# Expert weights in a ring of three thirds: two transfers of 6 MB an expert from one array, in place of three of 4 MB

## The chip, the cores and the metric

One core of one Trainium2 chip runs the whole layer. The metric is the device time in microseconds, the median over runs of the same kernel. MB stands here for 2^20 bytes, except in the profile's own rows, which count 10^6 bytes to a MB.

## What is computed

```python
n = rms_norm(x, norm1_w); proj = n @ w_in            # q, k, v and u: 256 tokens, width 1024
a = sliding_window_attention(q, k, v, sinks)         # 8 query heads, 2 key heads, window 128
p = multiscale_pool(u, pool_w, pool_scale)
h = x + concat(a, p) @ w_out
# mixture of experts: 32 experts, the best 4 for each token, all in float32
logits = rms_norm(h) @ w_router + b_router
gu = xb @ w_gu[e] + b_gu[e]                          # w_gu[e] 1024 x 2048
act = min(gate, 7) * sigmoid(1.702 * gate) * (clip(up, -7, 7) + 1)
y = act @ w_down[e] + b_down[e]                      # w_down[e] 1024 x 1024
h = h + segment_sum(y * gate_weight)
```

All 32 experts get tokens, so every weight is read once from HBM: 12 MB an expert, 384 MB in all, beside some 13 MB for the layer's first half.

## The kernel before

**Pieces and the ring.** An expert's weights are six pieces of 2 MB (`PIECES`), each 16 KB a partition: pieces 0 to 3 hold gate and up, 4 and 5 hold down. A gate-up piece is two chunks of 128 rows by 2048 columns, a down piece four chunks of 128 by 1024. The weights live in `ring`, which has 8 slots (`RING`), and piece number s (expert times 6 plus piece) goes to slot s mod 8. After the first three experts `load_pair` fills two slots with one transfer of 4 MB, 32 KB a partition, so an expert is three transfers: two from `w_gu`, one from `w_down`. SP (SyncE) issues all of them on one queue. Before each it waits on `pieces_used`, which TensorE raises when it has used up a piece: `load_pair(s)` needs `s + 2 - 8` pieces used.

**Loading ahead.** Buffers of the first half that are free early take parts of late experts (`ahead`): the first chunk of experts 24 to 29 (1 MB each; `AHEAD = 6`), four of the twelve half-MB blocks in the tile `extra`, and the first down chunk of experts 24 and 25 (`down_ahead`, 0.5 MB each). These experts' transfers are shorter by as much. In the first half of the program SP loads single pieces and halves of pieces as slots come free (`BY_CHUNK`, `SINGLES = 14`).

**TensorE's order.** `expert` does, for one expert of up to 64 tokens: `gate_up` (eight chunks, then the bias), `between` (gather of tokens for a later expert, `to_tokens`, which adds the last expert's result to the tokens' sums, `turn_round`, which transposes the activations once VectorE and ScalarE have made them, and `turn_gates`), and `down` (eight chunks). `wait_landed` stands at pieces 0, 2 and 4, one wait a transfer. Experts 0 to 3 are unrolled, then come eight short matmuls for the bias of down (line 1378), a loop of four experts run five times, and eight experts unrolled. The last two experts (30 and 31) are interleaved: both `gate_up` first, then both `down`, and SP loads them in that order (`LAST_TWO`) and, from piece 2 of expert 30 on, cut small (`END_CUTS`, each cut with a semaphore of its own, `landed_end`), down to 0.5 MB.

**The end.** After the last down chunk `to_tokens` of expert 31 closes the sums, ScalarE and VectorE copy them out and three transfers store them.

```python
            for s in range(RING + 2, 3 * TP - 2 * PIECES, 2):
                sp.wait_ge(pieces_used, (TURNS - 3) * TP + s + 2 - RING)
                gu_ahead = 0 <= s - TP < AHEAD * PIECES and s % PIECES == 0
                load_pair(s, NE - 3 * TURN, 2 * FF if gu_ahead else DM if s in (TP + GU_PIECES, TP + PIECES + GU_PIECES) else 0)
```

The functions that the diff touches, and what calls them:

Of the kernel before, what the change touches and what calls it, by code (L numbers as in the profile page):

```python
# [29 lines left out]
P = 128  # L30
SEQ, DM = 256, 1024
# [34 lines left out]
END_CUTS = {(2, 2): ((4, 6), (6, 8)), (3, 0): ((0, 2), (2, 4)), (3, 2): ((4, 6), (6, 7), (7, 8)),  # L66
            (2, 4): ((0, 2), (2, 4), (4, 6), (6, 7), (7, 8)), (3, 4): ((0, 2), (2, 4), (4, 6), (6, 7), (7, 8))}
# [5 lines left out]
AHEAD = 6  # L73
# [43 lines left out]
def laid_out(inputs):  # L117
# [8 lines left out]
    def one_by_one(a, stops):  # L126
# [29 lines left out]
        "w_gu": w_gu.reshape(NE, 2, 4, P, 2, 2, 2, FF // 4).transpose(0, 1, 3, 2, 5, 6, 4, 7).reshape(NE * 2, P, PAIR),  # L156
        "w_down": w_down.reshape(NE, 8, P, DM).transpose(0, 2, 1, 3).reshape(NE, P, PAIR),
# [4 lines left out]
def layer_kernel(nc, x_tok, x_dim, first, second, third, fixed, bands, w_qkv, w_u, w_mix, w_pool, b_gu, b_down,  # L162
                 w_gu, w_down, out):
    out_t = out.rearrange("b (t p) d -> (b t) p d", p=P)
    w_gu_k = w_gu.rearrange("s p n -> p s n")
    w_dn_k = w_down.rearrange("s p n -> p s n")

    with ExitStack() as ctx:
# [25 lines left out]
        extra = sb("extra", [P, 4, 1024])  # L194
# [17 lines left out]
        def cut(n, of=passing):  # L212
# [67 lines left out]
            mixA[:, :, :].rearrange("p h s -> p (h s)"), bias[:, 0, :], U[:, :, :].rearrange("p t n -> p (t n)"), bias[:, 1, :], passing[:, 0:1024],  # L280
            *(extra[:, n, :] for n in range(4)))]
# [3 lines left out]
        down_ahead = [mixP[:, :, :].rearrange("p g s -> p (g s)"), xT[:, FF:2 * FF]]  # L285
# [19 lines left out]
        landed_end = {(u, c, k): sem(f"landed_end{u}_{c}_{k}") for (u, c), parts in END_CUTS.items() for k, _ in parts}  # L305
        ld_aside = [sem(f"ld_aside{k}") for k in range(2)]
        ld_ahead = [sem(f"ld_ahead{u}") for u in range(AHEAD)]
        ld_wout, ld_bdn, ld_bgu = sem("ld_wout"), sem("ld_bdn"), sem("ld_bgu")
        ld_down_ahead = [sem(f"ld_down_ahead{u}") for u in range(2)]
        landed = [sem(f"landed{c}") for c in range(RING // 2)]  # L310
# [30 lines left out]
        gt_psum, gt_sb, y_sb = sem("gt_psum"), sem("gt_sb"), sem("y_sb")  # L341
        more_done = sem("more_done")
# [21 lines left out]
        def _(sp):  # L364
# [51 lines left out]
            def load_down_ahead(u):  # L416

                sp.dma_start(down_ahead[u], w_dn_k[:, NE - 2 * TURN + u, 0:DM]).then_inc(ld_down_ahead[u], 16)
# [1007 lines left out]
```

## Time and profile before

| | |
|---|---|
| median of 3 runs | 988.81 us (988.5 to 988.91) |
| the profiled execution's own time | 988.7 us |
| its span in the profile | 986.9 us |
| TensorE busy | 946.6 us, 96% |
| 16 DMA engines, mean busy share | 9 in tenths in 39 of 40 slices |
| VectorE, ScalarE busy | 202.9 us, 127.7 us |
| HBM read | 416.80 MB (of 10^6 bytes) |

Two resources are busy almost without a break, so a busy share alone does not tell which one sets the end. The span is 1.8 us shorter than the execution's own time; what lies around it does not change with the order of the work. In the rows, an engine with a q (SPq) is that engine's sequencer, and "DMA ring<-w_gu_dram" in a chain is the time from the issue of a transfer to its landing.

### The profile page before, as it was taken

The numbers are of one execution on the slowest core, as the hardware profiler recorded it, in microseconds if no ns is written. First come the engines' busy times: TensorE is split into PE (matmuls) and PEld (weight loads), VectorE is DVE, ScalarE is ACT, GpSimd is POOL, SyncE is SP. The second block draws the span as 40 slices with busy tenths as digits, with TensorE's granted clock in tenths as the row PEclk, the third lists the DMA queues.
The fourth block names the chain that finished last, engine by engine and source line by source line (L and its number), as shares of the span: only waits on it lengthen the run. The fifth ranks groups of instructions, "written<-read, shape, count | busy, mean of one in ns | idle before, by whom it ended". The sixth has DMA issues, their size and how long they took to land.

```text
span 986.9 us, 11112 instructions
## 1 busy us (share of the span) xinstructions
PE 946.6 (96%) x4508; PEld 382.4 (39%) x4508; DVE 202.9 (21%) x610; ACT 127.7 (13%) x346; POOL 14.0 (1%) x9
## 2 busy tenths in 40 slices
PE   9999999999999899898989989889989999999997
PEld 5545433333333334333333333333333333333432
DVE  4645121212111121210112121011212112111121
ACT  2433111011110111010011101001101110011101
POOL 0031000000000000000000000000000000000000
PEclk9999999999999999999999999999999999999999
DMA  9999999999999999999999999999999999999996
GB/s 374 426 423 398 412 429 434 432 430 428 432 431 429 436 430 430 434 432 429 434 433 426 437 432 428 437 430 429 436 429 431 432 429 430 431 433 430 422 422 272
DMA packets 23869, 418.27 MB, mean 424 GB/s; under 512 B 2912, under 2 KB 3296, under 8 KB 8224
## 3 DMA queue, kind: packets, MB, share of 16 engines
q1 hardware_dynamic: 23408, 417.20, 99.2%
q10 hardware_dynamic: 432, 0.66, 0.2%
q8 instruction: 21, 0.34, 0.1%
q14 instruction: 8, 0.07, 0.0%
HBM read 416.80 MB, written 1.05 MB: 423 GB/s over the span
## 4 chain that ended last, share of the span: by engine, by line
PE 63%; DMA 36%; DVE 1%; issue 0%; ACT 0%; SPq 0%; DVEq 0%
DMA ring<-w_gu_dram 33%; PE ps L1237 29%; PE ps L1342 14%; PE ps L1205 4%; PE ps L1189 4%; DMA ring<-w_down_dram 3%; PE ps L1066 3%; PE ps L997 2%; PE ps L1004 1%; PE ps L1293 1%; PE ps L1301 1%; PE ps L1013 0%; PE ps L1039 0%; PE ps L1058 0%; PE ps L1046 0%
## 5 line engine op out<-in xcount | busy, mean ns | idle before, releaser
L1237 PE MATMUL ps<-ring,passing 128*64 128x512 f32 x1008 | 229.1, 604 | 14.8 <-DMA ring<-w_gu_dram 14.8
L1237 PE MATMUL ps<-ring,PR 128*64 128x512 f32 x976 | 224.5, 608 | 16.4 <-DMA ring<-w_gu_dram 16.2
L1342 PE MATMUL ps<-ring,PT 128*64 128x512 f32 x984 | 218.3, 595 | 0.5 <-DMA ring<-w_down_dram 0.5
L952 DVE TENSOR_SCALAR xw<-ps 128x256 f32<-128x256 f32 x64 | 27.2, 425 | 650.0 <-PE ps L1237 650.0
L1237 PEld LDWEIGHTS ps<-ring,passing 128*64 128x64 f32 x1008 | 76.8, 139 | 158.3 <-issue 143.8
L1237 PEld LDWEIGHTS ps<-ring,PR 128*64 128x64 f32 x976 | 74.9, 140 | 157.0 <-issue 145.4
L1342 PEld LDWEIGHTS ps<-ring,PT 128*64 128x64 f32 x984 | 68.1, 137 | 129.6 <-issue 127.5
L652 ACT ACTIVATE xw<-xw 128x256 f32<-128x256 f32 x64 | 26.6, 416 | 484.5 <-DVE xw L952 484.5
L1205 PE MATMUL ps<-PT 64*128 64x512 f32 x248 | 69.7, 640 | 0.0
L1189 PEld LDWEIGHTS ps<-qk,X 128*128 128x128 f32 x512 | 59.6, 191 | 18.8 <-issue 18.8
L1189 PE MATMUL ps<-qk,X 128*128 128x128 f32 x512 | 65.7, 281 | 0.0
L647 ACT COPY PT<-ps 128x512 f32<-128x512 f32 x31 | 18.1, 585 | 202.7 <-PE ps L1342 202.7
L965 DVE COPY PT<-ps 128x512 f32<-128x512 f32 x31 | 21.4, 692 | 41.5 <-PE ps L1293 41.5
L953 DVE TENSOR_SCALAR ps<-ps 128x256 f32<-128x256 f32 x64 | 27.0, 423 | 0.0
L923 DVE TENSOR_SCALAR qk<-C,qk 128x128 f32<-128x128 f32 x66 | 19.9, 344 | 28.3 <-PE ps L1301 28.3
L1237 PE MATMUL ps<-bgs,oneh 96*64 96x512 bf16 x128 | 25.5, 380 | 0.0
L957 DVE SCALAR_TENSOR_TENSOR ps<-ps,xw 128x256 f32<-128x256 f32 x64 | 24.1, 423 | 0.0
L961 DVE TENSOR_TENSOR xw<-ps,xw 128x256 f32<-128x256 f32 x64 | 23.9, 415 | 0.0
L1205 PEld LDWEIGHTS ps<-PT 64*128 64x128 f32 x248 | 18.7, 184 | 11.1 <-issue 7.6
L1293 PEld LDWEIGHTS ps<-C,xw 128*128 128x128 f32 x128 | 13.4, 140 | 24.3 <-issue 23.2
L997 PE MATMUL ps<-ring,xw 128*128 128x512 f32 (+1 forms) x64 | 22.3, 512 | 0.0
L1293 PE MATMUL ps<-C,xw 128*128 128x128 f32 x128 | 21.0, 286 | 0.5 <-DVE xw L961 0.5
(198 smaller groups left out, 374.6 us busy)
## 6 DMA issues: line engine op xcount, KB each, us to landing
ring<-w_gu_dram SPq DMA_DIRECT2D x48, 4096.0 KB, 28.2
ring<-w_down_dram SPq DMA_DIRECT2D x25, 4096.0 KB, 29.7
ring<-w_gu_dram SPq DMA_DIRECT2D x14, 2048.0 KB, 14.2
ring<-w_gu_dram SPq DMA_DIRECT2D x6, 3072.0 KB, 23.2
ring<-w_down_dram SPq DMA_DIRECT2D x5, 2048.0 KB, 23.1
ring<-w_gu_dram SPq DMA_DIRECT2D x9, 1024.0 KB, 9.6
ring<-w_down_dram SPq DMA_DIRECT2D x8, 1024.0 KB, 25.9
ring<-w_down_dram SPq DMA_DIRECT2D x2, 3584.0 KB, 27.6
```

Source lines behind the costliest of these rows:

```text
L652: nc.scalar.activation(sg[:, b, :], gb[:, b, :], ACT.Sigmoid, scale=ALPHA).then_inc(sig_ready, 1)
L952: nc.vector.tensor_scalar(gb[:, b, :], gu[:, b, 0, :], LIMIT, None, ALU.min).then_inc(g_ready, 1)
L953: nc.vector.tensor_scalar(gu[:, b, 1, :], gu[:, b, 1, :], LIMIT, -LIMIT, ALU.min, ALU.max).then_inc(u_ready, 1)
L957: nc.vector.scalar_tensor_tensor(gu[:, b, 1, :], gu[:, b, 1, :], 1.0, gb[:, b, :], ALU.add, ALU.mult).then_inc(ug_ready, 1)
L961: nc.vector.tensor_tensor(gb[:, b, :], gu[:, b, 1, :], sg[:, b, :], ALU.mult).then_inc(act_ready, 1)
L997: last = mm(ps[:, bank, 0:w], tT[:, k, t * P:(t + 1) * P], wqkv[:, k, a:a + w], start=k == 0, stop=k == KC - 1)
L1066: last = mm(ps[:, ACC[t] + c, :], src[:, h, t * P:(t + 1) * P], wout[:, first + h, 512 * c:512 * c + 512], start=first == 0 and h == 0, st ...
L1189: last = mm(ps[:, bank, k * P:(k + 1) * P], X[:, t, (4 * h + k) * P:(4 * h + k + 1) * P], S1[:, t, :], start=k == 0 and t == 0, stop=t == ...
L1205: return [mm(ps[:, ACC[t] + j, :], GT[64 * j:64 * j + 64, t, :], ye[64 * j:64 * j + 64, :], start=False, stop=True, skip_group_check=True) ...
L1237: last = mm(ps[64 * j:64 * j + 64, GU + b, :], lhs, halves[j][:, 512 * b:512 * b + 512], start=start, stop=stop)
L1293: last = nc.tensor.transpose(ps[:, bank, r * P:(r + 1) * P], gb[:, r // 2, r % 2 * P:(r % 2 + 1) * P], ident)
L1342: last = mm(ps[64 * j:64 * j + 64, bank, :], at[:, k, 64 * (c - GU_PIECES):64 * (c - GU_PIECES) + 64], rows[:, 512 * j:512 * j + 512], sta ...
```

## The change

The ring has nine slots, in three thirds of 6 MB (48 KB a partition). `w_gu` and `w_down` are laid out as one array, `w_all`, whose row 2e holds pieces 0 to 2 of expert e and row 2e + 1 pieces 3 to 5. `load_part` fills a third with one transfer and needs `3 * (part + 1) - 9` pieces used. TensorE waits at pieces 0 and 3. The fill before the loop ends with single pieces 18 to 20 (`SINGLES = 12`), so part 7 (pieces 21 to 23) is the first whole third. The tile `extra` goes; `ahead` serves experts 26 to 29, and the two blocks of `down_ahead` now hold the first chunk of piece 3 of expert 26 (`later_ahead`). TensorE runs experts 0 and 1, a loop of twelve experts run twice, then the bias matmuls, then experts 26 to 31. The last down chunk of expert 31 is loaded, multiplied, copied and added to the tokens' sums in two column halves.

```diff
-RING = 8
+RING = 9
...
-LAST_TWO = [(2, c) for c in range(GU_PIECES)] + [(3, c) for c in range(GU_PIECES)] + [(u, c) for u in (2, 3) for c in range(GU_PIECES, PIECES)]
 PIECE = 4096
-PAIR = 2 * PIECE
-FIRST_FILL = (1, 2, 2, 3)
-BY_CHUNK, SINGLES = (RING, RING + 1, RING + 3), 14
-MORE_LANDINGS, LATER_LANDINGS = (3, 1, 3, 1), (1, 1, 1, 0)
-END_CUTS = {(2, 2): ((4, 6), (6, 8)), (3, 0): ((0, 2), (2, 4)), (3, 2): ((4, 6), (6, 7), (7, 8)),
...
+PART = 3
+TRIPLE = PART * PIECE
+SLOTS_OF = RING // PART
+HALVES = NE * 2
+FIRST_PLACE = (NE - 2) * PIECES
+LAST_TWO = [(e, c) for e in (NE - 2, NE - 1) for c in range(GU_PIECES)] + [(e, c) for e in (NE - 2, NE - 1) for c in range(GU_PIECES, PIECES)]
+BY_CHUNK, SINGLES = (RING, RING + 1, RING + 3), 12
+LANDINGS = (2, 3, 4, 4, 6, 3, 3)
+END_CUTS = {(NE - 2, 0): ((0, 4),), (NE - 2, 2): ((4, 6), (6, 8)), (NE - 1, 0): ((0, 2), (2, 4)), (NE - 1, 2): ((4, 6), (6, 7), (7, 8)),
+            (NE - 2, 4): ((0, 2), (2, 4), (4, 6), (6, 7), (7, 8)), (NE - 1, 4): ((0, 2), (2, 4), (4, 6), (6, 7))}
+LAST_COLUMNS = ((0, 256), (256, 512))
...
-AHEAD = 6
+AHEAD = 4
+AHEAD_FROM = NE - 2 - AHEAD
+ROUND_PARTS, ROUND_EXPERTS = 12, 12
...
-        "w_gu": w_gu.reshape(NE, 2, 4, P, 2, 2, 2, FF // 4).transpose(0, 1, 3, 2, 5, 6, 4, 7).reshape(NE * 2, P, PAIR),
-        "w_down": w_down.reshape(NE, 8, P, DM).transpose(0, 2, 1, 3).reshape(NE, P, PAIR),
+        "w_all": np.concatenate([w_gu.reshape(NE, 8, P, 2, 2, 2, FF // 4).transpose(0, 2, 1, 4, 5, 3, 6).reshape(NE, P, GU_PIECES * PIECE),
+                                 w_down.reshape(NE, 8, P, DM).transpose(0, 2, 1, 3).reshape(NE, P, (PIECES - GU_PIECES) * PIECE)],
+                                2).reshape(NE, P, 2, TRIPLE).transpose(0, 2, 1, 3).reshape(HALVES, P, TRIPLE),
...
-        extra = sb("extra", [P, 4, 1024])
...
-            *(extra[:, n, :] for n in range(4)))]
...
-        down_ahead = [mixP[:, :, :].rearrange("p g s -> p (g s)"), xT[:, FF:2 * FF]]
+        later_ahead = [mixP[:, :, :].rearrange("p g s -> p (g s)"), xT[:, FF:2 * FF]]
...
-            def load_pair(s, first=0, skip=0):
-
-                slot, e, c = s % RING, first + s // PIECES, s % PIECES
-                src, row = (w_gu_k, e * 2 + c // 2) if c < GU_PIECES else (w_dn_k, e)
-                load(slot, row, src, skip, PAIR).then_inc(landed[slot // 2], 16)
...
+            def load_part(part, skip=0, rounds=0):
+
+                slot = part % SLOTS_OF
+                load(rounds + part, slot, skip).then_inc(landed[slot], 16)
...
-            load_pair(0)
+            load_piece(0, stop=2 * PIECE)
             load_piece(RING + 2)
-            for n in range(8, 2 * AHEAD):
-                load_ahead(n)
+            load_piece(RING - 1)
...
-            load_down_ahead(0)
+            load_later_ahead(0)
-                    load_down_ahead(1)
+                    load_later_ahead(1)
...
-            for s in range(RING + SINGLES, RING + 2 + TP, 2):
-                sp.wait_ge(pieces_used, s + 2 - RING)
-                load_pair(s)
-            with sp.Fori(1, TURNS - 3) as r:
-                for s in range(RING + 2, RING + 2 + TP, 2):
-                    sp.wait_ge(pieces_used, r * TP + s + 2 - RING)
-                    load_pair(s, r * TURN)
-            for s in range(RING + 2, 3 * TP - 2 * PIECES, 2):
-                sp.wait_ge(pieces_used, (TURNS - 3) * TP + s + 2 - RING)
-                gu_ahead = 0 <= s - TP < AHEAD * PIECES and s % PIECES == 0
-                load_pair(s, NE - 3 * TURN, 2 * FF if gu_ahead else DM if s in (TP + GU_PIECES, TP + PIECES + GU_PIECES) else 0)
...
+            first_part = (RING + SINGLES) // PART
+            with sp.Fori(0, 3) as r:
+                for part in range(first_part, first_part + ROUND_PARTS):
+                    sp.wait_ge(pieces_used, r * (PART * ROUND_PARTS) + PART * (part + 1) - RING)
+                    load_part(part, rounds=r * ROUND_PARTS)
+            for part in range(first_part + 3 * ROUND_PARTS, HALVES - 4):
+                sp.wait_ge(pieces_used, PART * (part + 1) - RING)
+                begun = part >= 2 * AHEAD_FROM and (part % 2 == 0 or part == 2 * AHEAD_FROM + 1)
+                load_part(part, 2 * FF if begun else 0)
...
+                if (e, first_c) == (NE - 1, GU_PIECES):
+                    part, first, at = place_of(KC - 1)
+                    ends = ring[:, at:at + DM].rearrange("p (j n) -> p j n", j=2)
+                    rows = w_k[:, part, first:first + DM].rearrange("p (j n) -> p j n", j=2)
+                    for q, (a, b) in enumerate(LAST_COLUMNS):
+                        sp.dma_start(ends[:, :, a:b], rows[:, :, a:b]).then_inc(landed_cols[q], 16)
...
-            down_out(NE - 1, 0, GU + 1, ye_last)
+            act.wait_ge(pieces_used, NE * PIECES)
+            for done, (a, b) in zip((y_first, y_sb), LAST_COLUMNS):
+                nc.scalar.copy(ye_last[:, a:b], ps[:, GU + 1, a:b]).then_inc(done, 1)
...
-                    s = place(c)
-                    pair = s % RING // 2
-                    fills = FIRST_FILL[pair] + s // RING
-
-                    if not (isinstance(turn, int) and turn == 0) or s >= RING:
-                        fills += MORE_LANDINGS[pair]
-                    if not (isinstance(turn, int) and turn == 0) or s >= 2 * RING:
-                        fills += LATER_LANDINGS[pair]
+                    part = 2 * e + c // PART
                     if step == "more":
-                        fills -= (1, 1, 1, 2)[pair]
-                    pe.wait_ge(landed[pair], turn * (16 * TP // RING) + 16 * fills)
-
+                        pe.wait_ge(landed_more[c // PART], later * (16 * TURN) + 16 * (e + 1 - NE))
+                        return
+                    fills = sum(LANDINGS[m] if m < len(LANDINGS) else 1 for m in range(part % SLOTS_OF, part + 1, SLOTS_OF))
+                    pe.wait_ge(landed[part % SLOTS_OF], rounds * (16 * 2 * ROUND_EXPERTS // SLOTS_OF) + 16 * fills)
...
+                        begun = early is not None and c == 0 or early == 0 and c == PART
+                        if not last_two and not begun and c % PART == 0:
                             wait_landed(c)
...
-                        elif c == GU_PIECES and k == first_ahead:
-                            wait_landed(c)
...
 
-            for u in range(TURN):
-                if u == 1:
-                    pe.wait_ge(GdT_sb, 1)
-                expert(0, u, "first" if u == 0 else None)
-
+            expert(0, "first")
+            pe.wait_ge(GdT_sb, 1)
+            expert(1)
+            with pe.Fori(0, 2) as r:
+                for e in range(2, 2 + ROUND_EXPERTS):
+                    expert(e, rounds=r)
             pe.wait_ge(ld_bdn, 16)
-            pe.wait_ge(GdT_sb, 1)
             for t in range(T):
                 for c in range(2):
                     mm(ps[:, ACC[t] + c, :], GdT[c * NE:(c + 1) * NE, t, :], bdn[c * NE:(c + 1) * NE, :], start=False, stop=True, skip_group_check=True)
-            with pe.Fori(1, TURNS - 2) as r:
-                for u in range(TURN):
-                    expert(r, u)
-            for u in range(TURN):
-                expert(TURNS - 2, u, early=u)
-
-            for u in range(TURN - 2):
-                expert(TURNS - 1, u, early=TURN + u)
-            gate_up, between, _, _, down = expert(TURNS - 1, TURN - 2, "last but one")
+            for u in range(AHEAD):
+                expert(AHEAD_FROM + u, early=u)
...
-            pe.wait_ge(y_sb, NE)
             for t in range(T):
-                for last in to_tokens(t, GT_last, ye_last):
-                    last.then_inc(acc_final, 1)
+                for q, (a, b) in enumerate(LAST_COLUMNS):
+                    pe.wait_ge(*((y_first, 1), (y_sb, NE))[q])
+                    for j in range(2):
+                        last = mm(ps[:, ACC[t] + j, a:b], GT_last[64 * j:64 * j + 64, t, :], ye_last[64 * j:64 * j + 64, a:b],
+                                  start=False, stop=True, skip_group_check=True)
+                        if b == 512:
+                            last.then_inc(acc_final, 1)
```

Of the two orders, first **SP at the late experts**: before, its issues from expert 29 on. The names `w_gu_dram`, `w_down_dram` and `w_all_dram` are the weight arrays in HBM; 8192 columns are 4 MB, 12288 are 6 MB.

```order
L397 DMA ring<-w_gu_dram 128x6144 [waits pieces_used]
L397 DMA ring<-w_gu_dram 128x8192 [waits pieces_used]
L397 DMA ring<-w_down_dram 128x8192 [waits pieces_used]
L397 DMA ring<-w_gu_dram 128x8192 [waits pieces_used]
L397 DMA ring<-w_gu_dram 128x4096 [waits pieces_used]
L397 DMA ring<-w_gu_dram 128x4096
```

And now, the issues after the loop:

```order
L405 DMA ring<-w_all_dram 128x12288 [waits pieces_used] x9
L405 DMA ring<-w_all_dram 128x10240 [waits pieces_used] x3
L405 DMA ring<-w_all_dram 128x12288 [waits pieces_used]
L405 DMA ring<-w_all_dram 128x10240 [waits pieces_used]
L405 DMA ring<-w_all_dram 128x12288 [waits pieces_used]
L405 DMA ring<-w_all_dram 128x10240 [waits pieces_used]
L405 DMA ring<-w_all_dram 128x12288 [waits pieces_used]
L405 DMA ring<-w_all_dram 128x8192 [waits pieces_used]
L405 DMA ring<-w_all_dram 128x4096 [waits pieces_used]
L405 DMA ring<-w_all_dram 128x4096
```

Three transfers an expert have become two, and the short ones (10240 columns) are 5 MB. The cut transfers at the end stand as before, but for the last 0.5 MB, which comes in two column halves.

Second, **TensorE at one late expert**, from its first chunk, which is taken from the ahead buffers: expert 29 before,

```order
L1237 MATMUL ps<-extra,PR 64x512 [waits ld_ahead5,xe_sb]
L1237 MATMUL ps<-extra,PR 64x512 x3
L1237 MATMUL ps<-ring,PR 64x512 [waits landed3]
L1237 MATMUL ps<-ring,PR 64x512 x11
L1237 MATMUL ps<-ring,PR 64x512 [waits landed0,xe_sb]
L1237 MATMUL ps<-ring,PR 64x512 x11
```

and now expert 29 again (`ps` is PSUM, `PR` and `passing` hold the gathered tokens, `bias` and `passing` ahead blocks):

```order
L1243 MATMUL ps<-bias,PR 64x512 [waits ld_ahead3,xe_sb]
L1243 MATMUL ps<-passing,PR 64x512
L1243 MATMUL ps<-bias,PR 64x512
L1243 MATMUL ps<-passing,PR 64x512
L1243 MATMUL ps<-ring,PR 64x512 [waits landed1]
L1243 MATMUL ps<-ring,PR 64x512 x11
L1243 MATMUL ps<-ring,PR 64x512 [waits xe_sb]
L1243 MATMUL ps<-ring,PR 64x512 x7
L1243 MATMUL ps<-ring,PR 64x512 [waits landed2]
L1243 MATMUL ps<-ring,PR 64x512 x3
```

Before, TensorE waited for a transfer ahead of piece 0 (its second chunk), of piece 2 and, further down, of the down chunks. Now the second wait (`landed2`) stands ahead of piece 3, and none ahead of down.

Third, **TensorE behind the loop**: the bias matmuls (line 1378 before, 1385 now) stood ahead of expert 4, and now stand ahead of expert 26:

```order
L1379 REGISTER_ALU
L1379 COMPARE_AND_BRANCH
L1385 MATMUL ps<-PT 128x512 [waits ld_bdn]
L1385 MATMUL ps<-PT 128x512 x3
L1243 MATMUL ps<-spare,passing 64x512 [waits ld_ahead0,xe_sb]
```

## Rows read from the trace of the kernel before

**Rows 1.** The page: busy time, and DMA rate in 40 slices.

```profile
PE 946.6 (96%) x4508; PEld 382.4 (39%) x4508; DVE 202.9 (21%) x610; ACT 127.7 (13%) x346; POOL 14.0 (1%) x9
...
GB/s 374 426 423 398 412 429 434 432 430 428 432 431 429 436 430 430 434 432 429 434 433 426 437 432 428 437 430 429 436 429 431 432 429 430 431 433 430 422 422 272
```

**Rows 2.** Chain of waits, the middle: start us, us, what.

```profile
397.94 31.45 DMA ring<-w_gu_dram
429.43 7.53 PE ps L1237 x36
...
456.21 31.45 DMA ring<-w_gu_dram
```

**Rows 3.** Chain: an expert with no wait, bias matmuls, half a gate-up.

```profile
144.75 14.17 PE ps L1237 x68
...
160.91 1.06 PE ps L1205 x4
161.97 0.59 PE ps L1293 x4
...
163.61 0.37 PE ps L1301 x2
163.98 7.02 PE ps L1342 x32
171.00 14.17 PE ps L1237 x68
...
197.25 1.92 PE ps L1378 x8
...
848.86 6.89 PE ps L1237 x32
```

**Rows 4.** TensorE by time: start us, us, what [idle before, releaser].

```profile
908.98 6.23 PE L1237 MATMUL ps<-ring,PR 128*64 128x512 f32 x28 [0.27 <-DMA ring<-w_gu_dram]
...
928.79 13.10 PE L1237 MATMUL ps<-ring,passing 128*64 128x512 f32 x60 [0.21 <-DMA ring<-w_gu_dram]
...
946.16 7.09 PE L1237 MATMUL ps<-ring,passing 128*64 128x512 f32 x32
953.44 6.23 PE L1237 MATMUL ps<-ring,passing 128*64 128x512 f32 x28 [0.19 <-DMA ring<-w_gu_dram]
...
963.35 1.94 PE L1342 MATMUL ps<-ring,PT 128*64 128x512 f32 x8 [0.49 <-DMA ring<-w_down_dram]
...
970.90 1.94 PE L1342 MATMUL ps<-ring,xw 128*64 128x512 f32 x8 [1.23 <-DMA ring<-w_down_dram]
```

**Rows 5.** Chain of waits, the end.

```profile
901.88 26.77 DMA ring<-w_gu_dram
928.79 14.19 PE ps L1237 x66
...
979.42 2.83 PE ps L1205 x12
```

**Rows 6.** Single issues at 144.79, 171.04 and 956.47 us: KB, us to landing.

```profile
ring<-w_gu_dram SPq DMA_DIRECT2D x1, 2048.0 KB, 11.7
...
ring<-w_gu_dram SPq DMA_DIRECT2D x1, 4096.0 KB, 14.7
...
ring<-w_down_dram SPq DMA_DIRECT2D x1, 512.0 KB, 21.7
```

**Rows 7.** DMA totals of the stretches 400:600 and 124:160 us.

```profile
DMA packets 2953, 86.28 MB, mean 431 GB/s; under 512 B 320, under 2 KB 320, under 8 KB 320
...
DMA packets 1062, 15.39 MB, mean 427 GB/s; under 512 B 123, under 2 KB 123, under 8 KB 123
```

**Rows 8.** DMA rate in 40 slices of 982 to 984 us; a store issued at 982.13.

```profile
GB/s 0 0 328 0 0 0 0 0 0 0 0 0 0 0 0 0 0 0 0 492 328 246 492 492 328 246 573 410 82 655 410 164 655 328 246 492 410 410 246 655
```

**Rows 9.** Stretch 800:983: busy of each engine, granted clock, DMA share, GB/s.

```profile
800.00:983.00 183.00, 179.28 (x870) 68.30 (x866) 32.46 (x93) 19.89 (x51) 0.00 (x0) 1.00 0.96 411
```

**Rows 10.** Chain, an expert at 662 us: second half of gate and up.

```profile
662.54 9.22 PE ps L1237 x36
```

More of the change, by code:

```diff
@@ L305, in layer_kernel @@
         landed_end = {(u, c, k): sem(f"landed_end{u}_{c}_{k}") for (u, c), parts in END_CUTS.items() for k, _ in parts}
+        landed_cols = [sem(f"landed_cols{q}") for q in range(len(LAST_COLUMNS))]
         ld_aside = [sem(f"ld_aside{k}") for k in range(2)]
@@ L308, in layer_kernel @@
         ld_wout, ld_bdn, ld_bgu = sem("ld_wout"), sem("ld_bdn"), sem("ld_bgu")
-        ld_down_ahead = [sem(f"ld_down_ahead{u}") for u in range(2)]
-        landed = [sem(f"landed{c}") for c in range(RING // 2)]
+        ld_later_ahead = [sem(f"ld_later_ahead{j}") for j in range(2)]
+        landed = [sem(f"landed{c}") for c in range(SLOTS_OF)]
+        landed_more = [sem(f"landed_more{h}") for h in range(2)]
         split = sem("split")
@@ L399, in load_piece @@
             def load_piece(s, first=0, stop=PIECE):
-                e, c = s // PIECES, s % PIECES
-                src, row = (w_dn_k, e) if c >= GU_PIECES else (w_gu_k, e * 2 + c // 2)
-                load(s % RING, row, src, first, stop).then_inc(landed[s % RING // 2], 16)
-            def load_pair(s, first=0, skip=0):
-                slot, e, c = s % RING, first + s // PIECES, s % PIECES
-                src, row = (w_gu_k, e * 2 + c // 2) if c < GU_PIECES else (w_dn_k, e)
-                load(slot, row, src, skip, PAIR).then_inc(landed[slot // 2], 16)
+                part, base = s // PART, s % PART * PIECE
@@ L1352, in expert @@
                 if step == "more":
-                    if u % 2 == 0:
+                    if e % 2 == 0:
                         gather_own()
@@ L1378, in _ @@
                     mm(ps[:, ACC[t] + c, :], GdT[c * NE:(c + 1) * NE, t, :], bdn[c * NE:(c + 1) * NE, :], start=False, stop=True, skip_group_check=True)
-            with pe.Fori(1, TURNS - 2) as r:
-                for u in range(TURN):
-                    expert(r, u)
-            for u in range(TURN):
-                expert(TURNS - 2, u, early=u)
-            for u in range(TURN - 2):
-                expert(TURNS - 1, u, early=TURN + u)
-            gate_up, between, _, _, down = expert(TURNS - 1, TURN - 2, "last but one")
+            for u in range(AHEAD):
+                expert(AHEAD_FROM + u, early=u)
+            gate_up, between, _, _, down = expert(NE - 2, "last but one")
             gate_up()
             between()
-            gate_up, _, turn_round, turn_gates, down_last = expert(TURNS - 1, TURN - 1, "last")
+            gate_up, _, turn_round, turn_gates, down_last = expert(NE - 1, "last")
             gate_up()
```

117 lines of the change are left out of this document (59 added, 58 removed).

## The prediction, made before the changed kernel was run

> **What bounds the kernel now.** I read the page first: TensorE is busy for 96% of the span, and the DMA engines move 420 to 437 GB/s in nearly every slice [rows 1]. So the chain of waits has to say which of the two is ahead. In the middle of the program it shows the same picture expert after expert: TensorE runs until it comes to piece 2, and stands until a transfer lands. From the landing at 397.94 + 31.45 = 429.39 to the one at 456.21 + 31.45 = 487.66 are 58.27 us [rows 2], and 24 MB landed in them: 2.428 us a MB, 29.1 us an expert. An expert costs TensorE 171.00 - 144.75 = 26.25 us where it waits for nothing [rows 3]. The stream of weights sets the pace, and TensorE idles some 2.9 us an expert.
>
> The end is another matter, and the timeline shows it [rows 4]. From 800 us on TensorE is busy 179.28 of 183 us [rows 9]: experts 24 to 29 need only 11 MB or less of the stream, 26.7 us, as much as TensorE's 26.25. Its waits are 0.27, 0.21, 0.19, 0.49 and 1.23 us. The last weights land at 956.47 + 21.7 = 978.2 [rows 6], and the last matmul ends at 979.42 + 2.83 = 982.25 [rows 5]. Stream and TensorE arrive together, with about 2 us of slack in TensorE, so whatever makes TensorE later against the stream in the last experts moves the end. The profiled execution took 988.7 us, the median is 988.81: the sum below is made on 988.7. A measurement of this kernel can tell 0.2%, 2 us, from no change.
>
> **The change, part by part.**
>
> *The stream.* Every byte is still read once, so its length changes by packets and gaps only.
> (a) Rows of 48 KB. With 32 KB a partition the stream moves 86.28 million bytes in 200 us, with mostly 16 KB 15.39 million in 36 us [rows 7]: 2.431 and 2.453 us a MB, so 32 more rows a MB cost 0.022 us. 48 KB rows make 21.3 rows a MB, not 32: 0.0074 us a MB less. Up to the end of expert 25 there are 45 such transfers, 270 MB: -2.0 us. No row shows a row over 32 KB; were it moved as 32 + 16 KB, the sign turns, +2.0. I take the first, since the issue is one row of 12288 columns like the others; both ends go into the range.
> (b) Four half-MB blocks for `extra` become one piece: by the same price a few tenths, -0.2.
> (c) A gap. The last single piece, 20, is issued like the single at 144.79, when piece 11 is used up, and lands 11.7 later, at 156.5 [rows 6]. Part 7 needs piece 14 used, six chunks into expert 2: 144.75 + 6 x 6.89 / 4 = 155.1 [rows 3]. From the issue to the first bytes are 0.8 us: a store issued at 982.13 moves bytes from 982.95 [rows 8]. That just joins. Part 7's 6 MB take 14.6 us, to about 170.7. Part 8 needs the whole of expert 2 used, 171.00 [rows 3]; its bytes start at 171.9. Before, a transfer issued at 171.04 had 4 MB queued ahead of it and landed 14.7 later [rows 6], so there was no gap. Now it is 1.2 to 1.3 us. The next third is free at 181.3 and wanted at 186.5, and the margin grows from there to about 12 us. Bounds: 0 (the latency is shorter than I read) and 3. I take +1.3.
> Sum for the stream: -2.0 - 0.2 + 1.3 = -0.9 us.
>
> *TensorE's lag behind the stream.* This is the large term. Before, the third transfer of an expert held down alone, so when it landed, TensorE was at most 7 us of down and what it had in hand behind; it finished expert 29 at 928.6, as the first pair of expert 30 landed at 901.88 + 26.77 = 928.65 [rows 4, 5]. Now the second third holds piece 3 and both down pieces, and TensorE may begin piece 3 only when all 6 MB are there. What follows that landing is a quarter of gate and up with the bias (14.17 - 10.33 = 3.84), what stands between (26.25 - 14.17 - 7.02 = 5.06) and down (7.02): 15.9 us [rows 3]. In the middle this is covered: 15.9 + 10.3 for the next expert's pieces 0 to 2 is under 29.1. At the end it is not.
> The last stretch with a wait is expert 25. Between the end of its weights and the first pair of expert 30 come 10 MB for expert 26, 3 x 11 for 27 to 29, and 4: 47 MB, 114.1 us. So they land at 928.65 - 114.1 = 814.5. TensorE restarts 0.13 us after a landing and loses 0.25 more (7.53 against 14.17 - 6.89 = 7.28) [rows 2, 3]: 0.4 us. Then it runs 15.9, the bias matmuls, 1.92, which stood at 197.25, where TensorE had time to spare, and now stand here [rows 3], four experts at 26.25, 105.0, and the last two. Their work, without waits, is 14.19 + 3.16 (to 946.16) + 14.17 + 2 x 7.02 for down + 0.59 + 0.37 (turned) + 1.06 (tokens) + 2.83 = 50.4 [rows 3 to 5]. The end of the matmuls is 814.5 + 0.4 + 15.9 + 1.9 + 105.0 + 50.4 = 988.1, against 982.25: +5.8 us. To see that no transfer is waited for on the way: piece 3 of expert 29 is reached at 814.9 + 15.9 + 1.9 + 78.75 + 10.3 = 921.8, and its third landed at 928.65 - 9.7 = 918.9. The stream in turn isn't starved: the thirds it wants come free 6 us or more before.
> The lower bound of this term leaves out the lag gathered before expert 29: 918.9 + 0.4 + 15.9 + 50.4 = 985.6, +3.4 us. The upper one adds a fall of the clock: in one expert the half of gate and up took 9.22 us, not 7.53 [rows 10, 2], and one such near expert 25 costs 1.7. From 800 us on the granted clock was 1.00, full speed, 2.4 GHz [rows 9], and TensorE will be busier there, so I take none.
> The Trainium skill (Perfetto Trace Analysis, DMA Optimizations) says that splitting transfers "may allow some to start sooner", and that larger ones saturate HBM better. The trace agrees with both, and they pull apart here: the second is term (a), a row's price, and the first is this term.
>
> *The two column halves at the end.* They spare half of the last chunk, 7.02 / 16 = 0.4 us, after the last landing, but TensorE comes to it some 7 us after that landing, so they save nothing. Cost 0; if the stream were last, -0.3.
>
> *The rest.* TensorE's loop of twelve has the same instructions an expert; its cost is 0 while TensorE waits for the stream (2.9 us an expert), and if a turn of the loop cost 1 us in fetching code, that wait would cover it, but for the code behind the loop. VectorE and ScalarE do what they did, at 21 and 13% busy [rows 1].
>
> Sum: 988.7 - 0.9 + 5.8 = **993.6 us**, 0.5% slower.
>
> **The rivals.**
> *1, not slower: the lag is absorbed.* The place is piece 3 of expert 29. If the work from that landing to the end (0.4 + 15.9 + 50.4 = 66.7) were no longer than what the stream and its tail take (982.25 - 918.9 = 63.3), the end would stay with the last landing, and the stream's -0.9, the column halves' -0.3 and a little more of (a) would be left: 987.3. It decides below 63.3 us, so 3.4 us of TensorE's work would have to vanish. For it speaks only that 50.4 is a sum of pieces, against it that each piece is a row. 0.07.
> *2, faster: each transfer carries a fixed cost at the queue.* There are some 26 fewer large ones (53 thirds and two pairs for 81 pairs). Pairs at 2.431 and singles at 2.453 us a MB [rows 7] leave at most 4 x 0.022 = 0.09 us a transfer, 2.3 us in all, which (a) mostly holds already: 985.0 with rival 1 beside it, and slower than before without. 0.03. The Trainium skill (DMA: Bandwidth & Descriptors, Anatomy of one DMA) gives a transfer some 2 us fixed beside its bytes; paid in series that would be an estimated 52 us here, and a time near 942. By that rule, as a price in a full queue, the trace disagrees: 4 MB land every 9.7 us.
> *3, slower than forecast: the rows of 48 KB are cut in two, or the clock falls once, or the gap at part 8 is 3 us.* 993.6 + 4.0, + 1.7 or + 1.7: 995.3 to 997.6. 0.25.
>
> **How the numbers follow.** Forecast 0.65, rivals 0.07, 0.03 and 0.25. The forecast's own spread is the lag's +3.4 to +7.5 and the gap's 0 to 3: 991 to 996. The range takes that and rival 3: 990.8 to 997.4. Slower by over 0.2% is above 990.8: 0.65 + 0.25, less a little for the lag's lower bound with a longer gain in (a): 0.88. Within 0.2%: rival 1 and that little, 0.08. Faster: 0.04.
>
> **What would show it.** The last landing near 977 to 978, and matmuls without a DMA wait from about 815 us to the end; the last DMA wait of TensorE at piece 3 of expert 25; a wait of some 2.5 us an expert before that, at piece 3 alone; the end of the matmuls about 10 us behind the last landing, not 4; a dent in the DMA rate at 171 us; 48 KB rows seen as fewer packets and a rate slightly above 431 GB/s in the middle. The forecast is wrong if TensorE still waits for weights in the last two experts, or if the rate in the middle falls.

## The result, and the profile after

The changed kernel took 1000.59 us (median of 5 runs, 999.54 to 1003.96), the kernel before 988.91 beside it: a ratio of 1.0121, with a 95% interval of 1.0109 to 1.0132. It is slower, as forecast, but by 11.7 us where 4.9 were forecast, and outside the stated range. The profiled execution took 999.92 us, its span is 998.0.

The page of the changed kernel, the lines that answer to [rows 1], and the queues:

```profile
PE 953.0 (95%) x4520; PEld 377.7 (38%) x4520; DVE 202.9 (20%) x610; ACT 128.0 (13%) x347; POOL 14.0 (1%) x9
...
GB/s 373 428 426 397 411 427 370 432 432 426 430 440 433 424 432 440 432 426 430 437 430 428 432 438 430 430 431 436 432 428 432 436 427 426 410 429 428 423 420 181
...
q1 hardware_dynamic: 19344, 417.19, 98.1%
q8 instruction: 39, 0.64, 0.3%
```

The seventh slice of the rate (150 to 175 us) has fallen to 370 GB/s, where before it was 434. TensorE is busy 6 us longer in all, at a mean granted clock of 0.979 (0.987 before); from 800 us to the end of the matmuls it is 1.00, as before [rows 9]. The code queue (q8) moved 39 packets; it was 21 before.

The chain of waits at the end, which answers to [rows 5] (start us, us, what):

```profile
788.32 31.58 DMA ring<-w_all_dram
819.94 4.09 PE ps L1243 x20
...
836.11 1.92 PE ps L1385 x8
838.03 14.32 PE ps L1243 x68
...
943.16 14.19 PE ps L1243 x68
...
984.25 1.06 PE ps L1218 x4
...
991.67 1.78 PE ps L1408 x16
```

The last wait of TensorE for the stream is that at piece 3 of expert 25: the third lands at 788.32 + 31.58 = 819.90, and from there the chain is TensorE's, with the bias matmuls at 836.11, to 991.67 + 1.78 = 993.45. Before, it ended at 982.25.

Single issues of the changed kernel, at 144.9, 155.4, 171.3, 457.1, 467.4, 484.4 and 965.3 us, each with KB and us to landing, as in [rows 6]:

```profile
ring<-w_all_dram SPq DMA_DIRECT2D x1, 2048.0 KB, 11.5
...
ring<-w_all_dram SPq DMA_DIRECT2D x1, 6144.0 KB, 18.8
...
ring<-w_all_dram SPq DMA_DIRECT2D x1, 6144.0 KB, 19.1
...
ring<-w_all_dram SPq DMA_DIRECT2D x1, 6144.0 KB, 25.5
...
ring<-w_all_dram SPq DMA_DIRECT2D x1, 6144.0 KB, 31.3
...
ring<-w_all_dram SPq DMA_DIRECT2D x1, 6144.0 KB, 28.7
...
ring<-w_all_dram SPq DMA_DIRECT2D x1, 256.0 KB, 20.0
```

The last weights land at 965.29 + 20.0 = 985.3, before at 978.2: the stream is **7.1 us later**. The matmuls end 8.15 us behind it, before 4.0: TensorE's lag is **4.15 us more**. That is all of the 11.2.

Two of the other landings tell where the stream lost time. The single 20 lands at 144.9 + 11.5 = 156.4, part 7 at 155.4 + 18.8 = 174.2: 17.8 us for 6 MB that take 14.5 elsewhere. Part 8 lands at 171.3 + 19.1 = 190.5, 16.3 later. And in the middle, where no queue is dry, the landings at 482.6, 498.7 and 513.2 are 16.1 and 14.5 apart: a landing now and then is 1.4 to 1.6 us late, and what follows does not catch up. The stretches of the first kind (busy time of PE, PEld, DVE, ACT, POOL, then granted clock, DMA share, GB/s):

```profile
155.00:160.00 5.00, 5.00 (x31) 2.25 (x28) 1.66 (x5) 0.83 (x2) 0.00 (x0) 1.00 0.88 301
160.00:165.00 5.00, 5.00 (x30) 2.46 (x30) 2.64 (x8) 1.52 (x5) 0.00 (x0) 1.00 1.04 452
170.00:175.00 5.00, 5.00 (x26) 1.72 (x24) 0.00 (x0) 0.59 (x1) 0.00 (x0) 1.00 0.89 315
175.00:180.00 5.00, 5.00 (x26) 1.60 (x24) 0.00 (x0) 0.00 (x0) 0.00 (x0) 1.00 0.89 374
```

In 155 to 160 and in 170 to 180 the engines stand still for a part of the time. Finer, the rate from 154 to 158 us in 40 slices of 0.1 us, with a row's bytes in the slice in which it starts:

```profile
GB/s 164 492 492 164 328 328 164 328 164 0 164 0 0 0 164 0 0 0 0 0 0 0 0 0 2949 3441 983 0 0 492 0 0 0 0 0 0 0 0 0 0
```

One engine after another starts its last row of single 20, the last at 155.4. All 16 then begin part 7 together at 156.4 to 157.0, one microsecond after its issue. By their packets they had ended single 20 between 154.3 and 156.0, so they stood for 1.5 us in the mean, though part 7 was issued 1.0 us before single 20 had landed.

The second kind goes with code. In the stretch 300 to 770 us the kernel before has no packet on the code queue:

```profile
DMA packets 7009, 202.94 MB, mean 432 GB/s; under 512 B 784, under 2 KB 784, under 8 KB 784
## 3 DMA queue, kind: packets, MB, share of 16 engines
q1 hardware_dynamic: 7009, 202.94, 100.3%
issues: line engine op xcount, KB each, median us to landing
```

and the changed kernel has 18 of 16 KB:

```profile
DMA packets 4665, 203.20 MB, mean 432 GB/s; under 512 B 519, under 2 KB 519, under 8 KB 519
## 3 DMA queue, kind: packets, MB, share of 16 engines
q1 hardware_dynamic: 4647, 202.90, 100.0%
q8 instruction: 18, 0.29, 0.3%
```

### The profile page after: what moved, and what is told of

It reads as the page before. It is cut to its first block, busy times and chain, and to the rows that moved or that the text cites. A ratio compares the mean times of both kernels' runs of the same rounds, so it can differ in the third digit from the quotient of the medians.

```text
span 998.0 us, 11045 instructions
## 1 busy us (share of the span) xinstructions
PE 953.0 (95%) x4520; PEld 377.7 (38%) x4520; DVE 202.9 (20%) x610; ACT 128.0 (13%) x347; POOL 14.0 (1%) x9
## 4 chain that ended last, share of the span: by engine, by line
PE 65%; DMA 33%; issue 1%; DVE 0%; ACT 0%; SPq 0%
DMA ring<-w_all_dram 33%; PE ps L1243 31%; PE ps L1349 15%; PE ps L1202 4%; PE ps L1218 4%; PE ps L1079 3%; PE ps L1010 2%; PE ps L1017 1%; PE ps L1303 1%; PE ps L1311 1%; PE ps L1026 0%; PE ps L1052 0%; PE ps L1071 0%; PE ps L1059 0%; PE ps L1116 0%
## 5 line engine op out<-in xcount | busy, mean ns | idle before, releaser
L1243 PE MATMUL ps<-ring,passing 128*64 128x512 f32 x1000 | 232.5, 616 | 20.5 <-DMA ring<-w_all_dram 17.7
L1243 PE MATMUL ps<-ring,PR 128*64 128x512 f32 x992 | 229.5, 612 | 17.7 <-DMA ring<-w_all_dram 17.5
L1243 PEld LDWEIGHTS ps<-ring,passing 128*64 128x64 f32 x1000 | 73.2, 141 | 169.1 <-issue 141.9
L1243 PEld LDWEIGHTS ps<-ring,PR 128*64 128x64 f32 x992 | 72.6, 140 | 163.8 <-issue 135.5
L1202 PEld LDWEIGHTS ps<-qk,X 128*128 128x128 f32 x512 | 61.0, 195 | 18.8 <-issue 18.8
```

The lines of the kernel that those rows point to most:

```text
L1202: last = mm(ps[:, bank, k * P:(k + 1) * P], X[:, t, (4 * h + k) * P:(4 * h + k + 1) * P], S1[:, t, :], start=k == 0 and t == 0, stop=t == ...
L1243: last = mm(ps[64 * j:64 * j + 64, GU + b, :], lhs, halves[j][:, 512 * b:512 * b + 512], start=start, stop=stop)
```

## The experiments

My theory after the first look had three parts: a dry queue that costs more than its gap (part 7 and 8), TensorE's code loaded by the same DMA engines, since a loop of twelve experts is not kept, and the lag as predicted. The rival to each is that its loss belongs to the 48 KB rows, or to code behind the loop.

| label | kernel | us, median | ratio to before, 95% interval | last landing | end of matmuls |
|---|---|---|---|---|---|
| | before | 988.9 to 989.2 | | 978.2 | 982.3 |
| | changed | 1000.59 | 1.0121 (1.0109 to 1.0132) | 985.3 | 993.5 |
| e1 | before, loop written out | 992.04 | 1.0027 (1.0017 to 1.0036) | 981.2 | 985.3 |
| e2 | changed, fine fill | 997.49 | 1.0078 (1.0064 to 1.0091) | 980.3 | 989.4 |
| e3 | e2, bias early | 997.31 | 1.0080 (1.0066 to 1.0094) | 983.6 | 990.5 |
| e4 | changed, odd thirds in two | 998.22 | 1.0080 (1.0067 to 1.0094) | 986.2 | 992.9 |
| e5 | e2, all thirds in two | 996.24 | 1.0064 (1.0050 to 1.0078) | 985.4 | 989.3 |
| e6 | before, loop of eight | 992.54 | 1.0033 (1.0021 to 1.0046) | 981.9 | 985.9 |
| e7 | before, column halves | 989.58 | 1.0005 (0.9996 to 1.0014) | 979.0 | 982.9 |
| e8 | before, bias late | 989.24 | 0.9999 (0.9990 to 1.0008) | 978.5 | 982.6 |

The last two columns are of the profiled executions. The five runs of the changed kernel and of each of e2 to e5 spread over 1.3 to 4.4 us, those of e1 over 0.5, so the landings tell the parts apart better than the medians. They are those of one execution each, though, and a few tenths of them can be chance.

### e1: the kernel before, TensorE's loop written out

```diff
-            with pe.Fori(1, TURNS - 2) as r:
+            for r in range(1, TURNS - 2):
                 for u in range(TURN):
                     expert(r, u)
```

> The kernel before, with TensorE's loop of four experts (4 to 23) written out, nothing else. Theory (code loading): TensorE's code then no longer stays in its instruction buffer, so 16 KB of code an expert come over the DMA engines between 290 and 780 us, where the trace of before has none: some 18 more 16 KB packets, each holding up one engine by about 1.4 us (the excess at four landings of the changed kernel), over 8 engines: 18/8 x 1.4 = 3.2 us later last landing, 992 us. Rival (the lost time of the stream in the changed kernel is in the 48 KB rows or the thirds): 988.9, no change.

Measured: 992.04 us. The DMA totals of 300 to 770 us, and the issue of the last weights (KB, us to landing):

```profile
q1 hardware_dynamic: 6990, 202.35, 100.1%
q8 instruction: 16, 0.26, 0.2%
...
ring<-w_down_dram SPq DMA_DIRECT2D x1, 512.0 KB, 21.7
```

Sixteen code packets stand where before had none, 0.26 of 203 million bytes, and the last weights land at 959.51 + 21.7 = 981.2, 3.0 us later than before. The matmuls end 4.1 behind that, as before. With every transfer of weights, every wait and TensorE's work the same, code loading alone costs 3.0 us. The landings say where: in 300 to 770 us, where before has each 4 MB 9.71 us behind the last, six of e1's come 0.3 to 0.6 late, 2.9 us in all. In bytes the code would be 0.6 us of the whole stream, so it is not its size: the 16 engines end their shares of a transfer apart (in the changed kernel those of single 20 over 1.7 us), it has landed when the last one is through, and a code packet holds up one of them, for 1.07 us. That this is how 0.6 us become 3.0 is argued, not shown. My expectation had 3.2 by a sum over eight engines that no row here shows; that it came near is no proof of it.

### e6: the kernel before, a loop of eight experts

```diff
-            with pe.Fori(1, TURNS - 2) as r:
-                for u in range(TURN):
-                    expert(r, u)
+            with pe.Fori(0, 2) as r:
+                for v in range(2):
+                    for u in range(TURN):
+                        expert(r * 2 + (v + 1), u)
+            for u in range(TURN):
+                expert(TURNS - 3, u)
```

> The kernel before, with TensorE's loop over eight experts run twice and four experts written out, in place of four experts run five times. Theory (the code of the loop must stay in an instruction buffer): the trace shows whether 128 KB of code do. If not, code is loaded in all of the loop as in e1: 992, and some 38 code packets of 16 KB. If eight fit, packets come for the first pass and the four written out alone, some 8 more than before, 990. Rival (any loop is free of it): 989 and some 29 packets or fewer.

Measured: 992.54 us, like e1, and the page's code queue reads

```profile
q8 instruction: 39, 0.64, 0.3%
```

39 packets, as in the changed kernel, so a loop of eight is loaded again on every pass, and one of four is not. (The first pass of four is loaded: in before the packets end at 288.8 us and begin again at 780.8, behind the loop.) The changed kernel cannot have a shorter loop than twelve in this form: the ring's places repeat every three experts (18 pieces in 9 slots), the two buffers of gathered tokens every four.

### e2: the changed kernel, parts 7 and 8 as single pieces

```diff
+            for s in range(FINE[0] * PART, (FINE[-1] + 1) * PART):
+                part, base = s // PART, s % PART * PIECE
+                sp.wait_ge(pieces_used, s + 1 - RING)
+                load(part, part % SLOTS_OF, base, base + PIECE).then_inc(landed[part % SLOTS_OF] if s % PART == 2 else landed_fine[part], 16)
-            first_part = (RING + SINGLES) // PART
+            first_part = FINE[-1] + 1
```

> The changed kernel, with parts 7 and 8 loaded as six single pieces, each as its slot comes free, before whole thirds begin with part 9. Theory (a dry queue costs the gap and a slow common start of 16 engines): the excess of 3.2 us at the landing of part 7 and of 1.7 us at part 8 goes, 4.9 us in all: 995.7. Rival (the gap is 1.3 us as predicted, and the rest of the excess is code loading or something else at that time): 999.3.

Measured: the last landing is at 980.3, 4.9 us earlier than in the changed kernel, and 4.9 is the excess of parts 7 and 8. Over the two parts themselves e2 gains 4.7 us: its single 20 lands 1.0 later (157.4 against 156.4), its part 8 3.7 earlier (186.7 against 190.5). The other late landings fall differently in the two profiles, so that both numbers are 4.9 is partly chance. The same stretches as above, of e2:

```profile
155.00:160.00 5.00, 5.00 (x31) 2.38 (x28) 1.93 (x6) 0.83 (x2) 0.00 (x0) 1.00 1.02 433
170.00:175.00 5.00, 5.00 (x28) 1.59 (x24) 0.00 (x0) 0.59 (x1) 0.00 (x0) 1.00 1.01 429
```

The queue no longer runs dry. The time fell by less than the landing, to 997.49 (by 3.1, and by 3.7 in the profiled executions): the lag went from 8.15 to 9.1 us. The forecast had the engines standing for 1.3 us at part 8 and not at all at part 7. It had let a transfer end on all engines at once, and they fall idle one by one: at part 7 for 1.5 us in the mean (above), and at part 8, issued at 171.3 and 2.9 us before part 7 landed, from 171.5 on, with the next rows from 172.3. The rest lies in the start itself: the first rows of 48 KB took 1.9 to 3.5 us at part 7, 2.7 in the mean, and 2.0 to 3.2 at part 8, where one takes 1.82 in the full stream. Why they do is not shown.

### e3: e2 with the bias matmuls ahead of the loop

```diff
             expert(1)
+            pe.wait_ge(ld_bdn, 16)
+            for t in range(T):
+                for c in range(2):
+                    mm(ps[:, ACC[t] + c, :], GdT[c * NE:(c + 1) * NE, t, :], bdn[c * NE:(c + 1) * NE, :], start=False, stop=True, skip_group_check=True)
             with pe.Fori(0, 2) as r:
```

and the same lines taken out behind the loop.

> As e2, and the eight bias matmuls of down moved from behind the loop to ahead of it (ahead of expert 2). Theory (TensorE's lag from the landing of expert 25's last third to the end is all its work, with no wait): their 1.92 us go from the end: e2 less 1.9, 993.8. Rival (the end is set by the last landing and its tail): as e2, 995.7.

Measured: 997.31 us, no different from e2, and neither theory named the reason. The lag did fall, from 9.1 to 6.9 us, by the 1.9 us and a little. But the stream came 3.3 us later, 983.6: TensorE reaches every piece of experts 2 to 5 1.9 us later, frees its third as much later, and a new gap opens, in e3 at

```profile
198.00:206.00 8.00, 8.00 (x40) 2.60 (x37) 0.00 (x0) 0.58 (x1) 0.00 (x0) 1.00 0.81 302
```

0.81 of the engines' time, 302 GB/s. The landings at 202.5 and 218.5 are 1.5 us late each, 3.0 of the 3.3. The thirds were issued 3.3 and 3.4 us before the last one had landed; in e2 a third issued 3.9 us before came in time. The matmuls would have to stand where neither side is short, as they do before, ahead of expert 4; that was not run.

### e4: the changed kernel, the second third of each expert in two transfers

```diff
-                load(rounds + part, slot, skip).then_inc(landed[slot], 16)
+                if part % 2 == 0:
+                    load(rounds + part, slot, skip).then_inc(landed[slot], 16)
+                    return
+                load(rounds + part, slot, skip, PIECE).then_inc(landed[slot], 16)
+                load(rounds + part, slot, PIECE).then_inc(landed_down[slot], 16)
...
+                        if not last_two and c == GU_PIECES and k == 0:
+                            wait_down()
```

> The changed kernel, each second third of an expert (pieces 3 to 5) moved by two transfers, 2 MB and 4 MB, issued together when the third is free, with a wait of its own ahead of down. Theory (lag by the size of the transfer): TensorE begins piece 3 9.7 us sooner after expert 25, waits for the stream again in the last experts, and ends about 4.0 us behind the last landing in place of 8.2: 1000.6 - 4.2 = 996.4, a few tenths more for shorter rows. Rival (the end is late for another reason, such as code behind the loop): 1000.6 to 1001.

Measured: 998.22 us; in the profile, which is of the slowest of the five runs (999.78), the lag is 6.7 us, not 4.0, and TensorE does not meet the stream again. The chain (start us, us, what) says why:

```profile
774.60 32.71 DMA ring<-w_all_dram
...
807.44 16.09 PE ps L1254 x68
```

The wait that is left stands at expert 25's **first** third, still one transfer of 6 MB, which lands at 774.60 + 32.71 = 807.3. From there TensorE has 0.4 + 26.25 + 1.9 + 105.0 + 50.4 = 184.0 us of work, and so ends near 991.3; my expectation had looked at the second third alone. The 68 matmuls that follow took 16.09 us, not 14.17 [rows 3]: the granted clock stood at half, 1.2 GHz, for a part of them, after TensorE had stood for 1.96 us waiting for this third. The stretch 807 to 812 us, with a mean granted clock of 0.66:

```profile
807.00:812.00 5.00, 4.56 (x14) 1.78 (x16) 0.00 (x0) 0.00 (x0) 0.00 (x0) 0.66 1.02 436
```

The 1.9 us went to the end, 992.9. This is inconclusive on the size of the lag, and shows that it depends on both thirds, and that a fall of the clock behind the last wait is paid in full.

### e5: e2 with both thirds in two transfers

The even thirds go as 4 and 2 MB, the odd ones as 2 and 4, with four waits an expert:

```diff
-                load(rounds + part, slot, skip).then_inc(landed[slot], 16)
+                cut = PIECE if part % 2 else 2 * PIECE
+                load(rounds + part, slot, skip, cut).then_inc(landed[slot], 16)
+                load(rounds + part, slot, cut).then_inc((landed_down if part % 2 else landed_mid)[slot], 16)
...
+                        if not last_two and c == 2:
+                            wait_late(2 * e, landed_mid, {0: 6, 1: 4, 2: 8})
```

> As e2, and every third from part 4 on moved and waited for in two transfers as the kernel before does (4 and 2 MB, then 2 and 4 MB), issued together when the third is free; TensorE waits at pieces 0, 2, 3 and ahead of down. Theory (lag by the size of the transfer that TensorE waits for): TensorE is caught by the stream again in the last experts, and the matmuls end about 4 us behind the last landing, as before, not 9.0 as in e2's profile. The shorter rows cost the stream twice the 0.9 us that e4's last landing came later: last landing 982.2, end of the matmuls 986.3, time 993. Rival (the lag comes from code behind the loop or from the clock): 9 us behind the last landing still, 998.

Measured: 996.24 us. The chain at the end of e5:

```profile
946.68 31.17 DMA ring<-w_all_dram
...
977.99 1.94 PE ps L1372 x8
...
987.53 1.78 PE ps L1431 x16
```

A transfer is in the chain again (it lands at 946.68 + 31.17 = 977.85), and the matmuls end at 989.31, 3.9 us behind the last landing at 985.4, against 9.1 in e2. That fall alone would prove little: the matmuls of e2 end at 989.4 too, and the 5.1 us are those by which the stream is later. The gain is further up in the chain, at the start of expert 30, first e2, then e5:

```profile
939.12 14.19 PE ps L1251 x68
```

```profile
935.68 3.46 PE ps L1262 x16
```

TensorE gets there 3.4 us sooner, though the stream was 3.9 us later at expert 25 (its first third complete at 805.2, against 801.3) and a fall of the clock at 800.47 cost TensorE 1.9 us (16.09 for 14.17). From there the work without a wait is 50.3 us, as in e2, to 986.0, close to the 986.3 that I had expected; the late stream did the rest. This shows the lag as what it was taken for: the size of the transfer that TensorE waits for. The ring, the loop of twelve and the code behind it are those of e2. What I had wrong is the stream: it is 5.0 us later than in e2, not 1.9. The DMA totals of 400 to 600 us, first of e2, then of e5:

```profile
DMA packets 1986, 86.31 MB, mean 432 GB/s; under 512 B 224, under 2 KB 224, under 8 KB 224
```

```profile
DMA packets 3943, 85.84 MB, mean 429 GB/s; under 512 B 438, under 2 KB 438, under 8 KB 438
```

86.31 against 85.84 million bytes in 200 us, 0.54%, which over the 810 us from 170 on is 4.4 us. I had expected 1.9, from e4's last landing. The landings give the price: in the full stream a third lands every 14.53 us whole, and takes 9.71 + 4.90 = 14.61 as 4 and 2 MB, rows of 32 and 16 KB. Over some 45 thirds that is 3 us or a little more; 0.4 us stand at part 8 already, and 0.9 come late with one megabyte near the end, at 967.8: together some 4.5 of the 5.0. The kernel before is no counterexample: its 86.28 million bytes [rows 7] are (2953 - 320) rows of 32 KB and none of 16.

### e7 and e8: two small parts of the change, on the kernel before

e7 has the change's last step alone:

```diff
-                      (3, 4): ((0, 2), (2, 4), (4, 6), (6, 7), (7, 8))}
+                      (3, 4): ((0, 2), (2, 4), (4, 6), (6, 7))}
...
+                    if (u, c) == (3, GU_PIECES):
+                        for q, (a, b) in enumerate(LAST_COLUMNS):
+                            sp.dma_start(ends[:, :, a:b], rows[:, :, a:b]).then_inc(landed_cols[q], 16)
```

> The kernel before, with the change's last step alone: the last down chunk loaded, multiplied, copied and added in two column halves. Theory: the last landing comes 0.1 us later (1 KB rows), TensorE has half a chunk, 0.43 us, less to do behind it: 0.3 us faster, 988.9. Rival (rows of 1 KB or the extra copies cost more than that): 989.3 to 989.8.

Measured: 989.58, a ratio of 1.0005 (0.9996 to 1.0014): no change that can be told. A gain of 0.3 us would lie inside that interval too (0.03%), and is neither shown nor excluded. The last landing of its profile is 0.75 us later, the lag 0.1 us less.

e8 moves the bias matmuls alone to behind the loop:

```diff
-            pe.wait_ge(ld_bdn, 16)
-            pe.wait_ge(GdT_sb, 1)
-            for t in range(T):
-                for c in range(2):
-                    mm(ps[:, ACC[t] + c, :], GdT[c * NE:(c + 1) * NE, t, :], bdn[c * NE:(c + 1) * NE, :], start=False, stop=True, skip_group_check=True)
             with pe.Fori(1, TURNS - 2) as r:
```

(and the same lines ahead of `expert(TURNS - 2, u, early=u)`).

> The kernel before, with the change's move of the bias matmuls alone: from ahead of expert 4 to behind the loop (ahead of expert 24). Theory (behind the loop TensorE has no slack but the stream does not move): 1.92 us of work meet about 2 us of slack that the last waits show, and most of it is absorbed in steps: +0.3 to +1.9, 989.5 to 991. Rival (work ahead of expert 24 is still covered by the stream, TensorE waits there): 989.2, no change.

Measured: 989.24, ratio 0.9999 (0.9990 to 1.0008). In the kernel before the end is set by the last landing and TensorE's slack takes the 1.9 us; in the changed one, where TensorE sets the end, the same matmuls stand in the chain (836.11, 1.92).

None of these kernels is faster than the one before.

## Why the prediction was wrong

*What bounds the end: right.* TensorE was to run without a wait from expert 25's last third on. It did: the wait at 819.9 is its last for weights. From that landing to the end of the matmuls I worked out 0.4 + 15.9 + 1.9 + 105.0 + 50.4 = 173.6 us; the chain has 993.45 - 819.90 = 173.55, and its parts agree one by one (16.2 to the bias matmuls, 1.9, 105.1 and 50.3), so the match is not luck.

*(a) Rows of 48 KB: right in sign and size.* They are moved whole: 4665 packets in 300 to 770 us, not 7009. 6 MB land every 14.53 us, against 14.57 for the same bytes before (by the medians of the landings 14.534 and 14.570); over 45 transfers -1.6 us, where I had -2.0.

*(c) The gap: right place, wrong size. This is the first term that failed.* I counted the time from the end of one transfer, as if it ended on all engines at once, to the first byte of the next: 1.3 us at part 8 and none at part 7. The landings were 3.2 us late at part 7 and 1.7 at part 8, 4.9 in all, and e2 gave that back when the queue stayed full. Two things were missing: the 16 engines end apart, and stand until the next transfer is issued and 1.0 us more (0.8 in my sum), and their first rows are slow. My upper bound of 3 us was too low, and it had no row behind it.

*"The rest", the loop of twelve: this is the step that failed outright.* I priced the loop's code as a cost to TensorE, hidden while it waits for the stream. The turn does cost TensorE 2.85 us, and it is hidden:

```profile
479.80 4.46 PE L1349 MATMUL ps<-ring,PT 128*64 128x512 f32 x20
487.10 3.34 PE L1243 MATMUL ps<-ring,passing 128*64 128x512 f32 x8 [2.85 <-issue]
```

But code comes over the same DMA engines as the weights, and the stream was the bound. e1 gives it 3.0 us on the kernel before, without any other part of the change, and e6 3.7. The trace of before would have told: its code queue is silent in 300 to 770 us, and has a packet an expert where the code is written out.

*The lag: right in mechanism, 4.15 us measured where I had +5.8.* The two figures are taken at different places, and that is the difference. From expert 25's last third to the end of the matmuls the forecast held (above). From that third to the last landing I had 978.2 - 814.5 = 163.7 us of stream, and it was 985.3 - 819.9 = 165.4: 1.7 us of what the stream lost came behind expert 25, where TensorE is behind anyway and does not feel it. Read at expert 25 the sum closes: the stream is 819.9 - 814.5 = 5.4 us late there, where I had 0.9 early, and the lag adds its 5.8: 11.2, as measured.

The 7.1 us at the last landing come, from the experiments, to gap 4.9, code 3.0 and rows -1.6, in all 6.3. The 0.8 us left are in the landings too: from 195 us on the late ones of the changed kernel add up to 6.5 us, four of them 1.4 to 1.6 us each (308.2, 498.7, 718.2, 925.9), and those of before to 2.3. That is 4.2 more, where e1 gives 3.0. Why a late landing of the changed kernel is 1.4 us and more, and one of e1 0.3 to 0.6, is not shown. e2 to e5 tell that these parts don't simply add to the time, since a later stream is in part hidden by TensorE's lag, and an earlier one brings out more of it.

Of the rivals, the first (lag absorbed) and the second (a fixed cost for each transfer in a full queue) did not come: there are 26 fewer transfers, and the stream is later. The Trainium skill (DMA: Bandwidth & Descriptors, Anatomy of one DMA) gives a transfer that GpSimd issues some 2 us fixed beside its bytes. The transfers here go by SP's hardware queue, and in a full queue they show no such price: 6 MB a transfer land every 14.53 us, and at 4 MB a transfer the same bytes took 14.57. Of the third rival, which was to hold what is slower than forecast, only the gap took part. Code was no rival at all, and so the range was too narrow on that side. A fall of the clock reached the end in e4 alone. In e3 one stands in the chain as well (20 matmuls at 789.91 took 6.99 us, not 4.09), but without it TensorE would have waited for the landing at 818.9, to the same end.

Costed at nothing, and nothing that could be measured: the column halves (e7). The bias matmuls (e8) cost nothing in the kernel before, and 1.92 us where TensorE sets the end.

## What to carry to other kernels

Where a stream of weights is the bound, everything that shares its DMA engines is on the path: look at the code queue before unrolling or lengthening a loop, and ask which loops are now silent there. When transfers get larger, price three things apart: what longer rows save, how long the consumer must wait for the whole of a transfer at the end, and whether a slot comes free before the queue is empty, above all where the fill goes over from small transfers to large. A queue of 16 engines dries engine by engine, before the last transfer has landed: here a third issued 3.9 us ahead of that landing was in time, and those issued 3.4 us ahead or less were not. A consumer that keeps pace with its stream can be caught by any of them.

## What was not expected of the hardware

After its first pass a loop of four experts of TensorE's code runs with no packet on the code queue; eight or twelve load 16 KB an expert on every pass (21, 39 and 39 packets in the whole kernel). Some 16 more such packets, 0.13% of the bytes in their stretch, made the weights 3.0 us later, 0.3% (e1).

Thirds of 6 MB issued 1.0, 2.9, 3.3 and 3.4 us before the transfer ahead of them had landed came 3.2, 1.7, 1.5 and 1.5 us late (changed kernel and e3); one issued 3.9 us before came in time (e2).

In the full stream, without a late landing, 6 MB in rows of 48 KB land every 14.53 us (changed kernel, e2), 4 MB in rows of 32 KB every 9.71 (before, e5), and 2 MB in rows of 16 KB every 4.90 (e5): 2.42, 2.43 and 2.45 us a MB.

The first rows after a dry queue took up to 3.5 us, against 1.82 in the full stream, with the same 48 KB (changed kernel, part 7).
